# Stationary operands woven in pairs of blocks in a hybrid encoder layer

## Chip, cores and metric

The kernel runs on one core of a Trainium2 chip. The metric is the device time of one execution in microseconds.

## What is computed

One encoder layer over 512 tokens of width 1024 (two sequences of 256), all in float32: a token mixer of three branches, then a mixture of 16 experts of which each token uses two. Cut to its matrix products, the reference is

```python
z = x @ w_in + b_in                       # q, k, v, u_sg, v_sg, glu_a, glu_g
a = neighbourhood_attention(q, k, v, rpb) @ w_a_o
bb = (u * sv) @ w_b_o                     # u = gelu(u_sg); sv: position mixing of layer_norm(gelu(v_sg))
c = silu(layer_norm(depthwise_conv(glu_a * sigmoid(glu_g)))) @ w_c_o
g = sigmoid(x @ w_gate + b_gate)          # three gates of width 1024
merged = g[0] * a + g[1] * bb + g[2] * c
x = layer_norm(ALPHA * x + merged @ w_o + b_o)
...
for e in range(N_EXPERTS):
    h = silu(xt @ w_e1[e]) * (xt @ w_e3[e])
    y = y + gates[:, e:e + 1] * (h @ w_e2[e])
x = layer_norm(ALPHA * x + y)
```

## The kernel before

Every engine has its own program, written out by hand, and semaphores join them. All large products use float32 values split in two: `hi` is the value cast to the engine's float32r type, `lo` the rest, value minus `hi`. A product of two values takes three matmuls, written by `three` (lines 1842 to 1844): hi by hi, hi by lo, lo by hi. TensorE takes for each a stationary operand of 128 x 128, which a weight load (LDWEIGHTS) brings in, and a moving operand of 128 x 512, read from SBUF while the matmul runs.

Weights come in units of 128 x 1024 elements (512 KB). For each unit SyncE issues a transfer into a ring (`raw`, later with `raw_rows`, `raw_more`, `raw_late`: 24 slots), ScalarE casts it to `w_hi` (`cast_hi`, line 719), VectorE subtracts into `w_lo` (`cast_lo`, line 1055), and TensorE uses it in 24 matmuls (before the experts) or 6 (in them). There are three slots for split units, four in the expert stage, so that ScalarE waits for TensorE to finish with an earlier unit.

There are 64 + 8 units before the experts. In `features` (units 0 to 7 and 16 to 63: glu, q, k, u_sg, the three gates and the three branch projections) the weights are stationary, as blocks of 128 columns, and the tokens move (`xT`, `branch`). In `tokens` (units 8 to 15, v and v_sg; units 64 to 71, the output projection `w_o`, whose last three of four units per half are in `mix_out`; and all 192 units of the experts) the transposed tokens are stationary (`xT`, `mT`, `xgT`, `hT`) and the weights move. `first_units` is `features` for units 0 and 1.

An expert is 12 units: four of w_e1, four of w_e3 (`hidden`), four of w_e2 (`output`). Its 128 gathered token rows `xg` are turned by 8 transposes (line 2137) into two PSUM banks, from which ScalarE writes `xgT_hi` (`split_xg`, line 932) and VectorE `xgT_lo` (line 1541); `h` is turned by 4 (line 2152) and split into `hT_hi` and `hT_lo` (lines 943 and 1551). `keep_busy` (line 2097) runs spare matmuls while the router's results are awaited, `joint_slots` (line 2117) builds the lists of slots by small matmuls, and `form_sum` (line 2238) starts the last sum with float32 matmuls of the identity by `x1`.

The operands of the large matmuls start at multiples of 256 bytes (`LINE`). Before the change every one is laid out block after block, so that a stationary block is 128 elements in a row in each partition.

## Time and profile before

| | us |
|---|---|
| median of 3 runs | 778.98 |
| lowest and highest | 777.98, 779.29 |
| the profiled execution | 777.9 |
| its span | 776.1 |
| TensorE matmuls busy | 745.4 (96%) |
| weight loads busy | 616.5 (79%) |
| VectorE busy | 609.9 (79%) |
| ScalarE busy | 432.6 (56%) |

The span goes from the first instruction to the last; 1.8 us of the execution's own time lie around it. Matmuls are pipelined: a row's duration holds the way through the array too, so two neighbours overlap, and the pace of a stream is read from the starts. A weight load has rows of its own (PEld) and runs beside the matmul before it.

### The profile page before, as it was taken

How to read it: one execution, taken by the hardware profiler on the slowest of the kernel's cores; microseconds unless marked ns; L12 is line 12 of the kernel's file. 1: busy time of each engine (PE TensorE's matmuls, PEld its weight loads, DVE VectorE, ACT ScalarE, POOL GpSimd, SP SyncE). 2: the span in 40 equal slices, each digit the busy share in tenths (PEclk: the TensorE clock that was granted, in tenths of full speed). 3: DMA queues.
4: the chain of work that ended last, by engine and by line, in shares of the span. 5: the costliest groups of instructions: out<-in, count | busy, mean ns of one | idle time of the engine just before them, and what ended most of it. 6: DMA issues, size and time to landing. Idle time of an engine off the chain costs nothing.

```text
span 776.1 us, 10638 instructions
## 1 busy us (share of the span) xinstructions
PE 745.4 (96%) x3516; PEld 616.5 (79%) x3516; DVE 609.9 (79%) x827; ACT 432.6 (56%) x585; POOL 72.0 (9%) x96
## 2 busy tenths in 40 slices
PE   4999999999999999999999979999999999999995
PEld 3888877887888888888888857888888888888873
DVE  5799977777678857444348888999999999999977
ACT  5522235657322335422421456888888888888851
POOL 5000000000000000000011121111111111110314
PEclk9999999999999999999999989999999999999998
DMA  9744657232343452332388587999999999999682
GB/s 297 238 98 108 204 147 205 71 93 84 109 134 109 112 167 74 115 103 88 104 303 300 186 302 255 351 392 379 388 386 389 391 400 384 381 394 378 146 171 111
DMA packets 137489, 175.51 MB, mean 226 GB/s; under 512 B 15419, under 2 KB 75559, under 8 KB 137431
## 3 DMA queue, kind: packets, MB, share of 16 engines
q1 hardware_dynamic: 128896, 154.95, 58.8%
q0 software_dynamic: 7616, 19.34, 8.3%
q10 hardware_dynamic: 934, 0.69, 0.3%
q8 instruction: 23, 0.38, 0.2%
q14 instruction: 20, 0.16, 0.1%
HBM read 164.06 MB, written 19.11 MB: 236 GB/s over the span
## 4 chain that ended last, share of the span: by engine, by line
PE 85%; DVE 8%; DMA 2%; ACT 2%; SPq 2%; issue 1%; POOL 0%; DVEq 0%; ACTq 0%; POOLq 0%
PE bank L1842 25%; PE bank L1844 25%; PE bank L1843 25%; DVE w_lo L1055 2%; PE bank L2137 2%; DMA raw<-in_w_in_dram 2%; SPq L606 1%; DVE conv L1125 1%; DVE conv_odd L1125 1%; PE bank L2058 1%; PE bank L1837 1%; PE bank L2152 1%; PE bank L2238 1%; PE bank L1888 1%; PE bank L1904 1%
## 5 line engine op out<-in xcount | busy, mean ns | idle before, releaser
L1055 DVE TENSOR_TENSOR w_lo<-raw,w_hi 128x1024 fp32r<-128x1024 f32 x103 | 125.0, 1220 | 77.2 <-ACT w_hi L719 77.1
L719 ACT CAST w_hi<-raw 128x1024 fp32r<-128x1024 f32 x103 | 107.0, 1048 | 101.5 <-PE bank L1844 97.6
L1842 PE MATMUL bank<-xT_hi,w_hi 128*128 128x512 f32 x352 | 138.5, 393 | 2.7 <-DVE xT_lo L1093 1.5
L1844 PE MATMUL bank<-xT_hi,w_lo 128*128 128x512 f32 x352 | 137.1, 390 | 0.0
L1843 PE MATMUL bank<-xT_lo,w_hi 128*128 128x512 f32 x352 | 137.0, 389 | 0.0
L1842 PE MATMUL bank<-w_hi,xgT_hi 128*128 128x512 f32 x198 | 80.1, 405 | 1.0 <-issue 1.0
L1842 PEld LDWEIGHTS bank<-xT_hi,w_hi 128*128 128x128 f32 x352 | 66.1, 188 | 17.3 <-issue 3.1
L1844 PE MATMUL bank<-w_hi,xgT_lo 128*128 128x512 f32 x198 | 77.5, 391 | 0.0
L1843 PE MATMUL bank<-w_lo,xgT_hi 128*128 128x512 f32 x198 | 77.3, 390 | 0.0
L1844 PEld LDWEIGHTS bank<-xT_hi,w_lo 128*128 128x128 f32 x352 | 66.1, 188 | 14.0
L1843 PEld LDWEIGHTS bank<-xT_lo,w_hi 128*128 128x128 f32 x352 | 66.1, 188 | 13.4
L834 ACT ACTIVATE gate<-bank,vec 128x512 f32<-128x512 f32 x24 | 16.5, 689 | 83.2 <-PE bank L1844 83.2
L1055 DVE TENSOR_TENSOR w_lo<-raw_more,w_hi 128x1024 fp32r<-128x1024 f32 x40 | 48.2, 1221 | 5.7 <-ACT w_hi L719 5.4
L1055 DVE TENSOR_TENSOR w_lo<-raw_late,w_hi 128x1024 fp32r<-128x1024 f32 x40 | 48.2, 1220 | 4.1 <-ACT w_hi L719 3.9
L1125 DVE SCALAR_TENSOR_TENSOR conv<-conv_in,conv_col,conv 128x512 f32<-128x512 f32 x60 | 44.6, 744 | 0.0
L719 ACT CAST w_hi<-raw_more 128x1024 fp32r<-128x1024 f32 x40 | 41.2, 1049 | 4.5 <-PE bank L1844 4.5
L1844 PEld LDWEIGHTS bank<-w_hi,xgT_lo 128*128 128x128 f32 x198 | 37.2, 188 | 7.9
L1842 PEld LDWEIGHTS bank<-w_hi,xgT_hi 128*128 128x128 f32 x198 | 37.3, 188 | 7.8 <-issue 1.2
L719 ACT CAST w_hi<-raw_late 128x1024 fp32r<-128x1024 f32 x40 | 41.2, 1050 | 2.5 <-PE bank L1844 2.5
L1843 PEld LDWEIGHTS bank<-w_lo,xgT_hi 128*128 128x128 f32 x198 | 37.3, 188 | 6.6
L1125 DVE SCALAR_TENSOR_TENSOR conv_odd<-conv_in,conv_col,conv_odd 128x512 f32<-128x512 f32 x56 | 41.6, 744 | 0.0
L1055 DVE TENSOR_TENSOR w_lo<-raw_rows,w_hi 128x1024 fp32r<-128x1024 f32 x32 | 38.3, 1218 | 0.0
(289 smaller groups left out, 1530.9 us busy)
## 6 DMA issues: line engine op xcount, KB each, us to landing
raw_more<-in_w_e_dram SPq DMA_DIRECT2D x48, 512.0 KB, 7.0
raw<-in_w_e_dram SPq DMA_DIRECT2D x48, 512.0 KB, 7.9
raw_late<-in_w_e_dram SPq DMA_DIRECT2D x48, 512.0 KB, 7.1
raw_rows<-in_w_e_dram SPq DMA_DIRECT2D x48, 512.0 KB, 7.9
raw<-in_w_in_dram SPq DMA_DIRECT2D x28, 512.0 KB, 6.5
raw<-in_w_gate_dram SPq DMA_DIRECT2D x24, 512.0 KB, 3.7
y_scratch<-zeros SPq DMA_DIRECT2D x8, 512.0 KB, 5.3
raw<-in_w_o_dram SPq DMA_DIRECT2D x8, 512.0 KB, 3.8
```

The source lines that it names most:

```text
L606: sp.dma_start(v_win[:, seq, j, :], v_grid[:, WINDOW[j]:WINDOW[j] + KCOLS, :]).then_inc(v_windows, 16)
L719: act.copy(hi_slot(j), raw_slot(j)).then_inc(hi_cast, 1)
L834: act.activation(gate[:, n if n < 2 else r % 2, d, :], bank(name)[:], ACT.Sigmoid, bias=column(V_GATE + n * DC + 2 * r + d)).then_inc(free ...
L1055: dve.tensor_tensor(lo_slot(j), raw_slot(j), hi_slot(j).bitcast(F32), ALU.subtract).then_inc(lo_cast, 1)
L1125: o = dve.scalar_tensor_tensor(out=sum_, in0=shifted, scalar=conv_col[:, k, c:c + 1], in1=sum_, op0=ALU.mult, op1=ALU.add)
L1837: o = pe.transpose(bank(name)[:, k * P:(k + 1) * P], tile(k), ident)
L1842: pe.matmul(out, hi_l, hi_r, start=start, stop=False)
L1843: pe.matmul(out, hi_l, lo_r, start=False, stop=False)
L1844: return pe.matmul(out, lo_l, hi_r, start=False, stop=stop)
L1888: o = pe.matmul(bank(("attended", g))[:, j * P:(j + 1) * P], v_win[:, seq, j, hp * P:(hp + 1) * P], probsT[:, j * P:(j + 1) * P], start=Tr ...
L1904: o = pe.transpose(bank(name)[:, tokens_of(t)], x_in[:, t, c * P:(c + 1) * P], ident)
L2137: o = pe.transpose(psum[M_XT + half][:, k * P:(k + 1) * P], xg[:, q, c * P:(c + 1) * P], ident)
```

## The change

Each stationary operand is woven: of two neighbouring blocks of 128 x 128, block 0 takes the even elements of 256 and block 1 the odd ones. The tiles are declared `[pairs, 128, 2]` instead of `[blocks, 128]`, with the same bytes; `woven`, `chunk` and `by_chunk` give the views. Woven are the split weights of `features` (`is_stationary`), `mT_hi`, `xgT_hi`, `xgT_lo`, `hT_hi` and `hT_lo`. Not woven are `xT` (which moves in `features` and is stationary in units 8 to 15), `mT_lo`, and all weights that move. The casts and subtractions that write a woven tile write with a step of two elements and take their source in the old order; those of VectorE also read the `hi` part with that step. The number and the order of the instructions, their waits, and all transfers stay the same. The first of two woven blocks starts at a multiple of 256 bytes, the second 4 bytes further.

```diff
--- before.py
+++ after.py
@@ -233,8 +233,8 @@
     w_s = sb(first, "w_s_in", [4, P])
     first.close()
     late = ExitStack()
-    mT_hi = sb(late, "mT_hi", [DC, T], F32R, LINE)
-    mT_lo = sb(late, "mT_lo", [DC, T], F32R)
+    mT_hi = sb(late, "mT_hi", [DC // 2, T, 2], F32R, LINE)
+    mT_lo = sb(late, "mT_lo", [DC, T], F32R, LINE)
     branch_hi.append(sb(late, "branch2_hi", [WC, T], F32R))
     branch_lo.append(sb(late, "branch2_lo", [WC, T], F32R))
     gate = sb(late, "gate", [2, 2, T])
@@ -310,12 +310,12 @@
     y_last_hi = sb(over_xg, "y_last_hi", [D], F32R, LINE)
     over_xg.close()
     xg = sb(moe, "xg", [2, D])
-    xgT_hi = sb(moe, "xgT_hi", [2, DC, SLOTS], F32R, LINE)
-    xgT_lo = sb(moe, "xgT_lo", [2, DC, SLOTS], F32R, LINE)
+    xgT_hi = sb(moe, "xgT_hi", [2, DC // 2, SLOTS, 2], F32R, LINE)
+    xgT_lo = sb(moe, "xgT_lo", [2, DC // 2, SLOTS, 2], F32R, LINE)
     h_silu = sb(moe, "h_silu", [FF])
     h = sb(moe, "h", [FF])
-    hT_hi = sb(moe, "hT_hi", [4, SLOTS], F32R, LINE)
-    hT_lo = sb(moe, "hT_lo", [4, SLOTS], F32R, LINE)
+    hT_hi = sb(moe, "hT_hi", [2, SLOTS, 2], F32R, LINE)
+    hT_lo = sb(moe, "hT_lo", [2, SLOTS, 2], F32R, LINE)
     over_y = ExitStack()
     y_0 = sb(over_y, "y_0", [D])
     y_last_lo = sb(over_y, "y_last_lo", [D], F32R, LINE)
@@ -418,7 +418,7 @@
     out_stored = sem("out_stored")
-    last_hT_hi, last_hT_lo = xgT_hi[:, 0, 0:4, :], xgT_lo[:, 0, 0:4, :]
+    last_hT_hi, last_hT_lo = xgT_hi[:, 0, 0:2], xgT_lo[:, 0, 0:2]
     turned = [next_turned[:, 0], onehot[:, 1]]
     placed_hi, placed_lo = [y_next_hi, y_last_hi], [y_next_lo, y_last_lo]
@@ -510,6 +510,30 @@
     def lo_slot(j):
         s = j % SPLIT if j < U_MOE else (j - U_MOE) % M_SPLIT
         return w_lo[:, s, :] if s < SPLIT else w_lo_more[:, s - SPLIT, :]
+
+    def is_stationary(j):
+
+        return j < U_V or U_QK <= j < U_WO
+
+    def woven(slot):
+
+        return slot.rearrange("p (k n b) -> p k b n", b=2, n=P)
+
+    def split_of(slot, j):
+
+        return woven(slot) if is_stationary(j) else slot
+
+    def raw_of(j):
+
+        return raw_slot(j).rearrange("p (k b n) -> p k b n", b=2, n=P) if is_stationary(j) else raw_slot(j)
+
+    def chunk(tile, c):
+
+        return tile[:, c // 2, :, c % 2]
+
+    def by_chunk(tile):
+
+        return tile.rearrange("p k n b -> p k b n")
     def unit_of(slot, cols):
         return slot.rearrange("p (c n) -> p c n", n=cols)
@@ -716,7 +740,7 @@
                 act.wait_ge(unit_used, nth(j - M_SPLIT + 1, per, i))
             elif j >= SPLIT:
                 act.wait_ge(unit_used, nth(j - SPLIT + 1, per, i))
-            act.copy(hi_slot(j), raw_slot(j)).then_inc(hi_cast, 1)
+            act.copy(split_of(hi_slot(j), j), raw_of(j)).then_inc(hi_cast, 1)
@@ -838,7 +862,7 @@
             for c in (2 * r, 2 * r + 1):
                 act.wait_ge(merged_ready, c + 1)
-                act.copy(mT_hi[:, c, :], merged[:, c, :]).then_inc(merged_hi, 1)
+                act.copy(chunk(mT_hi, c), merged[:, c, :]).then_inc(merged_hi, 1)
         for r in range(4):
             for n in range(2):
@@ -929,8 +953,8 @@
         def split_xg(n, q):
             for half in range(2):
                 act.wait_ge(*m_filled(M_XT + half, n))
-                act.copy(xgT_hi[:, q, 4 * half:4 * half + 4, :],
-                         psum[M_XT + half][:].rearrange("p (c n) -> p c n", c=4)).then_inc(xg_hi, 1)
+                act.copy(by_chunk(xgT_hi[:, q, 2 * half:2 * half + 2]),
+                         psum[M_XT + half][:].rearrange("p (k b n) -> p k b n", k=2, b=2)).then_inc(xg_hi, 1)
         def silu(unit, n, h_before=None):
             act.wait_ge(unit_used, unit + 1)
@@ -940,7 +964,7 @@
         def split_hT(n, hT_hi=hT_hi[:]):
             act.wait_ge(*m_filled(M_HT, n))
-            act.copy(hT_hi.rearrange("p c n -> p (c n)"), psum[M_HT][:]).then_inc(hT_hi_done, 1)
+            act.copy(by_chunk(hT_hi), psum[M_HT][:].rearrange("p (k b n) -> p k b n", k=2, b=2)).then_inc(hT_hi_done, 1)
         def scale_y(unit, n, q, half):
@@ -1052,7 +1076,7 @@
         def cast_lo(j, per=0, i=None):
             dve.wait_ge(hi_cast, nth(j, per, i))
-            dve.tensor_tensor(lo_slot(j), raw_slot(j), hi_slot(j).bitcast(F32),
+            dve.tensor_tensor(split_of(lo_slot(j), j), raw_of(j), split_of(hi_slot(j).bitcast(F32), j),
                               ALU.subtract).then_inc(lo_cast, 1)
         def row_stats(x, t):
@@ -1080,9 +1104,10 @@
         dve.tensor_copy(conv_col[:].rearrange("p t c -> p (t c)"), bank("vectors")[:, V_ALL:V_ALL + TAPS * WC])
         dve.tensor_copy(vec[:], bank("vectors")[:, 0:V_ALL]).then_inc(frees("vectors"), 1)
         dve.wait_ge(*raw_there(0))
-        dve.tensor_copy(hi_slot(0), raw_slot(0)).then_inc(first_hi, 1)
+        dve.tensor_copy(woven(hi_slot(0)), raw_of(0)).then_inc(first_hi, 1)
         dve.wait_ge(first_hi, 1)
-        dve.tensor_tensor(lo_slot(0), raw_slot(0), hi_slot(0).bitcast(F32), ALU.subtract).then_inc(lo_cast, 1)
+        dve.tensor_tensor(woven(lo_slot(0)), raw_of(0), woven(hi_slot(0).bitcast(F32)),
+                          ALU.subtract).then_inc(lo_cast, 1)
         for c in range(DC):
             if c % 2:
                 dve.wait_ge(x0T_full, c + 1)
@@ -1299,7 +1324,7 @@
             for c in (2 * r, 2 * r + 1):
                 dve.wait_ge(merged_hi, c + 1)
-                dve.tensor_tensor(mT_lo[:, c, :], merged[:, c, :], mT_hi[:, c, :].bitcast(F32),
+                dve.tensor_tensor(mT_lo[:, c, :], merged[:, c, :], chunk(mT_hi, c).bitcast(F32),
                                   ALU.subtract).then_inc(merged_lo, 1)
         done = 80
@@ -1537,9 +1562,11 @@
         def split_xg(n, q):
             for half in range(2):
                 dve.wait_ge(xg_hi, n * 2 + (half + 1))
-                part_of = (slice(None), q, slice(4 * half, 4 * half + 4))
-                dve.tensor_tensor(xgT_lo[part_of], psum[M_XT + half][:].rearrange("p (c n) -> p c n", c=4),
-                                  xgT_hi[part_of].bitcast(F32), ALU.subtract).then_inc(psum_free[M_XT + half], 1)
+                part_of = (slice(None), q, slice(2 * half, 2 * half + 2))
+                dve.tensor_tensor(by_chunk(xgT_lo[part_of]),
+                                  psum[M_XT + half][:].rearrange("p (k b n) -> p k b n", k=2, b=2),
+                                  by_chunk(xgT_hi[part_of].bitcast(F32)),
+                                  ALU.subtract).then_inc(psum_free[M_XT + half], 1)
         def gate_h(unit, n):
             dve.wait_ge(unit_used, unit + 1)
@@ -1548,8 +1575,8 @@
         def split_hT(n, hT_hi=hT_hi[:], hT_lo=hT_lo[:]):
             dve.wait_ge(hT_hi_done, n + 1)
-            dve.tensor_tensor(hT_lo.rearrange("p c n -> p (c n)"), psum[M_HT][:],
-                              hT_hi.rearrange("p c n -> p (c n)").bitcast(F32),
+            dve.tensor_tensor(by_chunk(hT_lo), psum[M_HT][:].rearrange("p (k b n) -> p k b n", k=2, b=2),
+                              by_chunk(hT_hi.bitcast(F32)),
                               ALU.subtract).then_inc(psum_free[M_HT], 1)
         make_joint(0, 0)
@@ -1846,13 +1873,13 @@
         def features(j, outs, x_hi, x_lo, per=0, i=None):
             pe.wait_ge(lo_cast, nth(j + 1, per, i))
-            hi, lo = unit_of(hi_slot(j), len(outs) * P), unit_of(lo_slot(j), len(outs) * P)
+            hi, lo = woven(hi_slot(j)), woven(lo_slot(j))
             chunks = UNIT // (len(outs) * P)
             for d, name in enumerate(outs):
                 open_bank(name, i)
-                cols = slice(d * P, (d + 1) * P)
                 for c in range(chunks):
-                    o = three(bank(name)[:], hi[:, c, cols], lo[:, c, cols], x_hi[:, c, :], x_lo[:, c, :],
+                    at = (slice(None), *divmod(len(outs) * c + d, 2))
+                    o = three(bank(name)[:], hi[at], lo[at], x_hi[:, c, :], x_lo[:, c, :],
                               c == 0, c == chunks - 1)
             o.then_inc(unit_used, 1)
@@ -1862,7 +1889,7 @@
             hi, lo = unit_of(hi_slot(j), 512), unit_of(lo_slot(j), 512)
             for t, out in enumerate(outs):
                 for c in range(2):
-                    o = three(out, choose(x_hi[:, 2 * k + c, :], t), choose(x_lo[:, 2 * k + c, :], t), hi[:, c, :],
+                    o = three(out, choose(x_hi(2 * k + c), t), choose(x_lo(2 * k + c), t), hi[:, c, :],
                               lo[:, c, :], k == 0 and c == 0, last and c == 1)
             o.then_inc(unit_used, 1)
@@ -1892,6 +1919,15 @@
         def in_row(x, t):
             return x[:, tokens_of(t)]
+        def whole(x, t):
+            return x
+
+        def chunks_of(tile):
+            return lambda c: chunk(tile, c)
+
+        def rows_of(tile):
+            return lambda c: tile[:, c, :]
+
         pe.wait_ge(const_loaded, 16)
         def turn_x0(t, chunks):
@@ -1923,10 +1959,10 @@
             name = ("glu_g" if u else "glu_a", 0)
             if chunks[0] == 0:
                 open_bank(name)
-            hi, lo = unit_of(hi_slot(u), P), unit_of(lo_slot(u), P)
+            hi, lo = woven(hi_slot(u)), woven(lo_slot(u))
             for c in chunks:
                 pe.wait_ge(*drained(("x0T", c)))
-                o = three(bank(name)[:], hi[:, c, :], lo[:, c, :], xT_hi[:, c, :], xT_lo[:, c, :], c == 0,
+                o = three(bank(name)[:], hi[:, c // 2, c % 2], lo[:, c // 2, c % 2], xT_hi[:, c, :], xT_lo[:, c, :], c == 0,
                           c == DC - 1)
             if chunks[-1] == DC - 1:
                 o.then_inc(unit_used, 1)
@@ -1946,12 +1982,14 @@
                 if u == U_V:
                     for t in range(TT):
                         open_bank(("v", t))
-                tokens(u, u - U_V, u == U_V + 3, [bank(("v", t))[:] for t in range(TT)], xT_hi, xT_lo, in_row)
+                tokens(u, u - U_V, u == U_V + 3, [bank(("v", t))[:] for t in range(TT)],
+                       rows_of(xT_hi), rows_of(xT_lo), in_row)
             elif u < U_QK:
                 if u == U_VSG:
                     for t in range(TT):
                         open_bank(("vsg", t))
-                tokens(u, u - U_VSG, u == U_VSG + 3, [bank(("vsg", t))[:] for t in range(TT)], xT_hi, xT_lo, in_row)
+                tokens(u, u - U_VSG, u == U_VSG + 3, [bank(("vsg", t))[:] for t in range(TT)],
+                       rows_of(xT_hi), rows_of(xT_lo), in_row)
             elif u < U_USG:
                 features(u, [("k" if u % 2 else "q", (u - U_QK) // 2)], xT_hi, xT_lo)
             else:
@@ -2014,8 +2052,8 @@
                 open_bank(("mixed", n, t))
             for k in range(1 if n else 4):
                 pe.wait_ge(merged_lo, 2 * k + 2)
-                tokens(U_WO + 4 * n + k, k, k == 3, [bank(("mixed", n, t))[:] for t in range(TT)], mT_hi, mT_lo,
-                       in_row)
+                tokens(U_WO + 4 * n + k, k, k == 3, [bank(("mixed", n, t))[:] for t in range(TT)],
+                       chunks_of(mT_hi), rows_of(mT_lo), in_row)
         def mix_out(t):
@@ -2025,7 +2063,7 @@
                 pe.wait_ge(lo_cast, j + 1)
                 hi, lo = unit_of(hi_slot(j), 512), unit_of(lo_slot(j), 512)
                 for c in range(2):
-                    o = three(bank(name)[:], in_row(mT_hi[:, 2 * k + c, :], t), in_row(mT_lo[:, 2 * k + c, :], t),
+                    o = three(bank(name)[:], in_row(chunk(mT_hi, 2 * k + c), t), in_row(mT_lo[:, 2 * k + c, :], t),
                               hi[:, c, :], lo[:, c, :], False, k == 3 and c == 1)
             if t < TT - 1:
                 o.then_inc(fills(name), 1)
@@ -2143,7 +2181,7 @@
                 pe.wait_ge(*m_empty(b, n))
             if k % 2 == 0:
                 pe.wait_ge(*m_drained(M_XT + k // 2, n))
-            tokens(j, k, k == 3, [psum[b][:]], xgT_hi[:, q], xgT_lo[:, q], lambda x, t: x, per, i)
+            tokens(j, k, k == 3, [psum[b][:]], chunks_of(xgT_hi[:, q]), chunks_of(xgT_lo[:, q]), whole, per, i)
         def turn_h(n):
             pe.wait_ge(*m_empty(M_HT, n))
@@ -2158,7 +2196,7 @@
                 pe.wait_ge(*m_drained(M_HT, n))
             if k % 2 == 0:
                 pe.wait_ge(*m_empty(M_Y + k // 2, n))
-            tokens(j, k % 2, k % 2 == 1, [psum[M_Y + k // 2][:]], hT_hi, hT_lo, lambda x, t: x, per, i)
+            tokens(j, k % 2, k % 2 == 1, [psum[M_Y + k // 2][:]], chunks_of(hT_hi), chunks_of(hT_lo), whole, per, i)
         pe.wait_ge(routed, 1)
         joint_slots(0, 0)
```

## Rows read from the trace of the kernel before

**Rows 1.** The page: busy time of each engine; chain that ended last, by line

```profile
PE 745.4 (96%) x3516; PEld 616.5 (79%) x3516; DVE 609.9 (79%) x827; ACT 432.6 (56%) x585; POOL 72.0 (9%) x96
...
PE bank L1842 25%; PE bank L1844 25%; PE bank L1843 25%; DVE w_lo L1055 2%; PE bank L2137 2%; DMA raw<-in_w_in_dram 2%; SPq L606 1%; DVE conv L1125 1%; DVE conv_odd L1125 1%; PE bank L2058 1%; PE bank L1837 1%; PE bank L2152 1%; PE bank L2238 1%; PE bank L1888 1%; PE bank L1904 1%
```

**Rows 2.** Grouped instructions of TensorE: busy us, mean ns, idle before

```profile
L1842 PE MATMUL bank<-xT_hi,w_hi 128*128 128x512 f32 x352 | 138.5, 393 | 2.7 <-DVE xT_lo L1093 1.5 <-DVE vs L1217 1.0 <-DVE w_lo L1055 0.2
...
L1842 PEld LDWEIGHTS bank<-xT_hi,w_hi 128*128 128x128 f32 x352 | 66.1, 188 | 17.3 <-issue 3.1 <-DVE w_lo L1055 0.6 <-DVE xT_lo L1093 0.5
L2152 PEld LDWEIGHTS bank<-const,h 128*128 128x128 f32 x64 | 8.0, 141 | 2.1
```

**Rows 3.** Timeline of TensorE matmuls, 301 us: start, duration, instruction

```profile
300.69 0.39 PE L1843 MATMUL bank<-xT_lo,w_hi 128*128 128x512 f32 x1
...
302.28 0.39 PE L1844 MATMUL bank<-xT_hi,w_lo 128*128 128x512 f32 x1
```

**Rows 4.** Timeline of TensorE weight loads, same stretch

```profile
302.28 0.19 PEld L1842 LDWEIGHTS bank<-xT_hi,w_hi 128*128 128x128 f32 x1
```

**Rows 5.** Stretches: length, busy by engine, granted clock, DMA share, GB/s

```profile
300.00:303.00 3.00, 3.00 (x15) 2.48 (x14) 3.00 (x3) 0.00 (x0) 0.00 (x0) 1.00 0.07 15
463.20:465.70 2.50, 2.50 (x7) 1.98 (x6) 2.50 (x3) 0.00 (x0) 1.56 (x1) 0.50 0.57 167
```

**Rows 6.** Timeline of TensorE matmuls, 463 us

```profile
463.20 3.37 PE L2097 MATMUL bank<-w_hi 128*128 128x512 f32 x8
```

**Rows 7.** Timeline of TensorE matmuls, last sum

```profile
757.58 1.02 PE L2238 MATMUL bank<-x,const 128*128 128x512 f32 x2
...
759.82 0.59 PE L2238 MATMUL bank<-x,const 128*128 128x512 f32 x1
```

**Rows 8.** Timelines of TensorE at 474 us, matmuls, then weight loads

```profile
475.11 0.40 PE L1843 MATMUL bank<-w_lo,xgT_hi 128*128 128x512 f32 x1
...
476.51 0.39 PE L1843 MATMUL bank<-w_lo,xgT_hi 128*128 128x512 f32 x1
...
473.98 0.86 PEld L2117 LDWEIGHTS bank<-info,onehot 128*128 128x128 f32 x7
474.76 0.19 PEld L1842 LDWEIGHTS bank<-w_hi,xgT_hi 128*128 128x128 f32 x1
```

**Rows 9.** Timeline of TensorE matmuls, 483 us

```profile
483.53 0.39 PE L1843 MATMUL bank<-w_lo,xgT_hi 128*128 128x512 f32 x1
483.76 0.40 PE L1844 MATMUL bank<-w_hi,xgT_lo 128*128 128x512 f32 x1
...
485.83 0.39 PE L1842 MATMUL bank<-w_hi_more,xgT_hi 128*128 128x512 f32 x1
...
486.73 0.39 PE L1843 MATMUL bank<-w_lo_more,xgT_hi 128*128 128x512 f32 x1
```

**Rows 10.** Stretches of the first stage and the expert stage

```profile
20.00:125.00 105.00, 103.92 (x463) 85.91 (x464) 90.33 (x132) 33.71 (x42) 1.90 (x2) 1.00 0.58 164
500.00:550.00 50.00, 50.00 (x241) 41.66 (x239) 46.51 (x49) 42.71 (x52) 5.06 (x5) 1.00 1.03 386
```

**Rows 11.** Chain of waits, expert stage: turns of xg

```profile
513.21 0.87 PE bank L2137 x8
...
530.90 0.88 PE bank L2137 x8
```

**Rows 12.** Grouped instructions of VectorE and ScalarE

```profile
L1055 DVE TENSOR_TENSOR w_lo<-raw,w_hi 128x1024 fp32r<-128x1024 f32 x103 | 125.0, 1220 | 77.2 <-ACT w_hi L719 77.1
L1541 DVE TENSOR_TENSOR xgT_lo<-bank,xgT_hi 128x512 fp32r<-128x512 f32 x32 | 20.4, 676 | 0.0
...
L719 ACT CAST w_hi<-raw 128x1024 fp32r<-128x1024 f32 x103 | 107.0, 1048 | 101.5 <-PE bank L1844 97.6 <-DMA raw<-in_w_in_dram 3.9
L932 ACT CAST xgT_hi<-bank 128x512 fp32r<-128x512 f32 x32 | 17.2, 590 | 17.0 <-PE bank L2137 17.0
```

## The prediction

> **What bounds the kernel now.** I read the page first: TensorE is busy 96% of the span, and of the chain that ended last a quarter of the span lies on each of the three matmuls of `three` [rows 1]. So time is saved only by a shorter pace of these matmuls. The change touches none of their number, shape or order; it changes how their stationary operand lies in SBUF. All hangs on one question: does the weight load, which runs beside the matmul before it, cost that matmul anything?
>
> The grouped rows give a load of 188 ns beside a matmul of 393 ns [rows 2], but both overlap their neighbours, so a group's mean says nothing of the pace. The timeline does. In a steady stretch (300.69 to 302.28 us) seven matmuls start 1.59 us apart from first to last, 0.227 us each [rows 3], and each load starts as a matmul starts [rows 4]. 512 columns at 2.4 GHz, which is the clock granted there (1.00) [rows 5], are 213.3 ns. So 13.3 ns per matmul are something else, 6% of the pace.
>
> Two more stretches tell what it is. At the granted clock 0.50 (1.2 GHz) eight matmuls of the same form take 3.37 us; less the last one's 0.39, seven starts are 0.426 us apart, just 512/1.2, though loads run beside them too [rows 5, 6]. At full clock a pair of F32 matmuls of 512 columns (line 2238) lasts 1.02 us against 0.59 for one: 0.43 apart, twice 0.215, so two passes at the full rate of columns with nearly nothing on top [rows 7]. Both of these take their moving elements from SBUF half as fast. Thus the 13.3 ns are no fixed price of changing weights: they come only when the moving operand is read at full speed and a load reads beside it. The two reads hinder each other.
>
> How much they hinder is a matter of their position in time. After small matmuls seven of the same shape start 1.40 us apart from first to last, 0.233 each [rows 8]. Elsewhere, also behind small matmuls (the turns of h), the four steps from 485.83 to 486.73 take 0.225 each again [rows 9]. Operands and bytes are alike, so this is no toll per load; collisions of two moving pointers fit it.
>
> A load's own reading time: where small matmuls are bound by their loads (line 2117, seven of them, then the next matmul's), seven loads go by from 473.98 to 474.76, 0.11 us each [rows 8]; the 188 ns of a row are that and a latency. In 0.11 us a load reads 128 elements of 4 bytes, 4.8 bytes per ns; the matmul reads 4 bytes per 0.417 ns, 9.6 bytes per ns. The moving pointer overtakes the load's all the time.
>
> **The change, part by part.** *Woven loads.* `features` takes a woven stationary operand in 56 units of 24 matmuls, 1344 (1056 of them on xT, three times the 352 of [rows 2]); the output projection in 8 units of 24, but only for mT_hi, two of each three, 128; the experts in 192 units of 6, 1152. Sum 2624, of them 1472 before the expert stage. The 192 in which xT itself is stationary stay as they are. A woven load passes over 1,024 bytes in the same 0.11 us: 9.6 bytes per ns, the very speed of the moving pointer. Two pointers at one speed keep their distance. If they collide at the start the stalled one falls back and they are apart for the rest. I therefore forecast that most of the 13.3 ns goes. The floor is 214 ns, nearly the bare 512 columns, as in the passes of [rows 7]; the ceiling on this view is the 0.227 of now. I take 216, two ns above the floor for the first collision: 10.7 ns saved.
>
> No row shows a woven load, so I bound it. Below: 214, which is 12.7 x 2624 = 33 us less. Above: the nearest load at an equal pace is that of a turn (line 2152), contiguous but 141 ns long instead of 188 [rows 2]: 47 ns less of about 110, so it reads some 8 to 9 bytes per ns. The matmul that it runs beside, at 483.76, is 0.40 long where those before it are 0.39 [rows 9]: up to some 10 ns dearer, I take 6, so 19 ns of toll in little more than half the reading time. This row speaks against me, and it is the price of the rival below.
>
> *Before the expert stage*: 1472 x 10.7 = 15.8 us, all on the chain; DVE has 90.3 of 105 us in the busiest stretch and would have 90.3 of 100 (463 matmuls start there) [rows 10].
>
> *Expert stage*: an expert takes 17.69 us (turns of xg at 513.21 and 530.90) [rows 11]. 72 x 10.7 ns = 0.77 makes it 16.92. DVE is busy 46.5 of 50 us [rows 10], 0.93 to 0.94; 0.94 x 17.69 = 16.6 us per expert. That just fits, but each subtraction waits for ScalarE's cast and that for TensorE to free a slot, so DVE is late next. Of 1152 x 10.7 = 12.3 us I count 10. The transfers keep up: of ScalarE's idle time before its casts the group of ring `raw` names 3.9 us of waiting for a unit to land, and those from w_in alone [rows 12].
>
> *Writers.* ACT's cast (1048 ns) and DVE's subtraction (1220 ns) of 56 units of stationary weights now write, and DVE also reads, every second element; so do xgT (590 and 676 ns) and hT [rows 12]. No row has a step of two. Below: nothing, as a gain would need more than one element at a time from operands that lie worse than now. Above: twice the time per element, (1220 - 676)/512 = 1.06 ns each more. In 20 to 125 us eleven such units would add 12 us to DVE's 90 of 105, still hidden; per expert three splits of 512 would add 1.6 us to DVE's 16.6, which would stand out by 0.5 us, 8 us in all. I take nothing: these rows show one element at a time and nothing that a neighbour could save. The order of instructions, the waits, the DMAs and SBUF sizes stay as they are.
>
> Sum: 15.8 + 10 = 26 us. The profiled execution took 777.9 us, 752 after; the median of the runs is 1.1 us above it, so **753 us**.
>
> **The rivals.** *The load's reads are the toll (slower).* 512 contiguous bytes cost 13.3 ns. If each stretch of SBUF that a load opens stalls the matmul, a woven load opens twice as many: 26.6 ns, pace 240, 13.3 x 2624 = 35 us more, 814. By the turn's row, 19 ns in about half the time, it could be near 40 ns, 850. For it: the turn's row, and that the steady toll is so constant. Against it: equal loads cost 0.233 or 0.227 by position [rows 8, 9]. It decides from any pace above 227. The Trainium skill (SBUF — State Buffer, Door 1, the note on cachelines) says that SBUF is read in lines of 16 bytes and that each access that crosses to a new line pays, with at least two hits per line wanted. A woven load has two hits where it had four, so by that page it is at the edge of being free and may well pay here; the toll fits 32 lines per load, but no row tells lines from elements.
>
> *No meeting at all (no change).* The toll may follow the number of elements, or be part of handing over at full clock; then 227 stays and the time is 779. For it: elements and load count are unchanged. Against it: the 0.426 and 0.43 of the half-rate stretches [rows 6, 7]. The Trainium skill (TensorE: Matmul & The Clock Gate, Part 2, step 1) gives the engine two independent read ports and says that a load steals no read bandwidth from the running matmul: by that rule weaving does nothing. The 13.3 ns disagree with it.
>
> *Never settled (slower).* At equal speed a bad distance may be kept too, and the pace stay in the mix of [rows 8], 0.233: 6 x 2624 = 16 us more, 794.
>
> *The writers become the bound:* 8 us more, 787.
>
> **How the numbers follow.** Forecast 0.45, its own range 745 to 773 (214 ns to a saving of a few ns). No change 0.15. Toll doubled 0.28, never settled 0.09, writers 0.03. Faster is thus 0.45, the same 0.15, slower 0.40, where 0.2% (1.6 us) is about what a measurement tells from none. The range 747 to 816 leaves out 0.04 below and about half of the toll's case, 0.14, above.
>
> **What would show it.** Right: starts of woven matmuls 0.214 to 0.218 apart, while those with contiguous operands (`tokens` on xT, 192 of them) stay at 0.227; an expert of 16.9 to 17.1 us with DVE at 97% or more; load rows still 188 ns. Wrong: a pace of 0.227 everywhere (no meeting), of 0.240 or more in the woven ones alone (toll), or casts above 1.1 us for ACT and 1.3 us for DVE in woven units.

## The result and the profile after

| | before | after |
|---|---|---|
| median, us | 778.95 | 795.33 |
| lowest and highest | 777.98, 779.29 | 794.87, 795.59 |
| the profiled execution | 777.9 | 795.1 |
| its span | 776.1 | 793.3 |

The ratio is 1.0212, with a 95% interval of 1.0194 to 1.0229: the change costs 16.4 us. The table's time before is the median of four runs. The forecast was 753 us, 26 less than before. Its sign is wrong. The range (747 to 816) holds the result only because it was drawn wide enough for the rivals.

The page of the kernel after, TensorE's line and the chain that ended last by line (the three matmuls of `three` are now lines 1869 to 1871):

```profile
PE 762.3 (96%) x3516; PEld 634.4 (80%) x3516; DVE 611.3 (77%) x827; ACT 438.4 (55%) x585; POOL 71.8 (9%) x96
...
PE bank L1869 27%; PE bank L1871 27%; PE bank L1870 27%; PE bank L2175 2%; PE bank L2096 1%; PE bank L1864 1%; PE bank L2190 1%; PE bank L2276 1%; PE bank L1915 1%; DVE w_lo L1079 1%; PE bank L1940 1%; DMA x_in<-in_x_prompt_dram 1%; PE bank L1905 1%; PE bank L2135 1%; ACT w_hi L743 1%
```

As in [rows 1] TensorE is busy 96% of the span and the three lines hold 81% of it on the chain, where it was 75. The counts of instructions are those of before. Its busy time is 16.9 us longer, nearly the 17.2 us of the span: the whole loss is TensorE's own time.

The grouped rows of the same execution, matmuls and loads:

```profile
L1869 PE MATMUL bank<-xT_hi,w_hi 128*128 128x512 f32 x352 | 140.4, 399 | 3.1 <-DVE xT_lo L1118 1.8 <-DVE vs L1242 1.1 <-DVE w_lo L1079 0.2
...
L1869 PEld LDWEIGHTS bank<-xT_hi,w_hi 128*128 128x128 f32 x352 | 68.3, 194 | 17.8 <-issue 3.5 <-DVE w_lo L1079 0.6 <-DVE xT_lo L1118 0.4
```

Matmuls went from 393 to 399 ns in the first form [rows 2], and a load row from 188 to 194. What stands ahead of them as idle time is the same (2.7 us, now 3.1): no new wait.

The pace is read from starts. The timeline of TensorE's matmuls in three stretches: woven weights in `features`; `tokens` on xT, whose stationary operand the change left alone; and the experts, with woven xgT and hT.

```profile
302.74 0.39 PE L1869 MATMUL bank<-xT_hi,w_hi 128*128 128x512 f32 x1
...
305.77 0.40 PE L1870 MATMUL bank<-xT_lo,w_hi 128*128 128x512 f32 x1
...
80.11 0.39 PE L1869 MATMUL bank<-w_hi,xT_hi 128*128 128x512 f32 x1
...
83.96 0.39 PE L1871 MATMUL bank<-w_hi,xT_lo 128*128 128x512 f32 x1
...
499.66 0.40 PE L1870 MATMUL bank<-w_lo,hT_hi 128*128 128x512 f32 x1
...
504.79 0.39 PE L1871 MATMUL bank<-w_hi,xgT_lo 128*128 128x512 f32 x1
```

The first two rows are 13 starts apart, 3.03 us: **0.233 us** each, where [rows 3] have 0.227. The next two are 17 starts apart, 3.85 us: 0.2265, as before. The last are 22 apart, 5.13 us: 0.233. So the matmuls with woven loads got slower, by some 6.7 ns each, and those on xT did not. Over the whole trace, taking every pair of neighbours that follow each other at once, the mean step went from 227.2 to 233.4 ns in `features` on xT, from 227.8 to 233.9 in the experts' matmuls on xgT (three of four weight slots), and from 226.8 to 235.3 in those on hT, the dearest; on xT as the stationary operand it is 226.7 both times.

Two stretches (columns as in [rows 5]) and, from the chain of waits, the turns of xg:

```profile
20.00:125.00 105.00, 103.91 (x453) 85.91 (x454) 89.57 (x128) 33.67 (x40) 1.91 (x2) 1.00 0.57 162
500.00:550.00 50.00, 50.00 (x234) 42.09 (x233) 45.75 (x47) 42.00 (x51) 6.07 (x6) 1.00 1.02 371
```

```profile
505.18 0.87 PE bank L2175 x8
523.40 0.87 PE bank L2175 x8
```

The clock is granted in full (1.00) in both, as before. In the same 105 us 453 matmuls start instead of 463, in the expert stage 234 instead of 241 [rows 10]. An expert takes 18.21 us instead of 17.69 [rows 11]: 0.52 more, over its 72 matmuls 7.2 ns each. VectorE's share fell (46.51 to 45.75 us of 50): it has more slack, not less.

The writers of the woven operands, grouped:

```profile
L1079 DVE TENSOR_TENSOR w_lo<-raw,w_hi 128x1024 fp32r<-128x1024 f32 x103 | 125.2, 1222 | 84.5 <-ACT w_hi L743 83.5
L743 ACT CAST w_hi<-raw 128x1024 fp32r<-128x1024 f32 x103 | 111.4, 1091 | 102.8 <-PE bank L1871 99.3 <-DMA raw<-in_w_in_dram 3.5
L956 ACT CAST xgT_hi<-bank 128x512 fp32r<-128x512 f32 x32 | 18.4, 634 | 18.4 <-PE bank L2175 18.4
```

Against [rows 12]: VectorE's subtractions do not feel a step of two (1220 to 1222 ns, 676 to 679). ScalarE's casts do a little: 590 to 634 for xgT, and 1048 to 1091 in a group of which about half is woven, so some 80 ns for a woven unit (an estimate, 43 ns x 103 / 56). In 20 to 125 us ScalarE is busy 34 of 105 us, in the expert stage 42 of 50, so that this stays hidden.

### The profile page after: what moved, and what is told of

Read it like the earlier page. It is cut to its first block, busy times and chain, and to the rows that moved or that the text cites. A ratio compares the mean times of both kernels' runs of the same rounds, so it can differ in the third digit from the quotient of the medians.

```text
span 793.3 us, 10638 instructions
## 1 busy us (share of the span) xinstructions
PE 762.3 (96%) x3516; PEld 634.4 (80%) x3516; DVE 611.3 (77%) x827; ACT 438.4 (55%) x585; POOL 71.8 (9%) x96
## 4 chain that ended last, share of the span: by engine, by line
PE 92%; DVE 4%; ACT 2%; issue 1%; DMA 1%; POOL 0%; ACTq 0%; DVEq 0%; POOLq 0%
PE bank L1869 27%; PE bank L1871 27%; PE bank L1870 27%; PE bank L2175 2%; PE bank L2096 1%; PE bank L1864 1%; PE bank L2190 1%; PE bank L2276 1%; PE bank L1915 1%; DVE w_lo L1079 1%; PE bank L1940 1%; DMA x_in<-in_x_prompt_dram 1%; PE bank L1905 1%; PE bank L2135 1%; ACT w_hi L743 1%
## 5 line engine op out<-in xcount | busy, mean ns | idle before, releaser
L1079 DVE TENSOR_TENSOR w_lo<-raw,w_hi 128x1024 fp32r<-128x1024 f32 x103 | 125.2, 1222 | 84.5 <-ACT w_hi L743 83.5
L743 ACT CAST w_hi<-raw 128x1024 fp32r<-128x1024 f32 x103 | 111.4, 1091 | 102.8 <-PE bank L1871 99.3
L1869 PE MATMUL bank<-xT_hi,w_hi 128*128 128x512 f32 x352 | 140.4, 399 | 3.1 <-DVE xT_lo L1118 1.8
L1871 PE MATMUL bank<-xT_hi,w_lo 128*128 128x512 f32 x352 | 139.0, 395 | 0.0
L1870 PE MATMUL bank<-xT_lo,w_hi 128*128 128x512 f32 x352 | 138.9, 395 | 0.0
L1869 PEld LDWEIGHTS bank<-xT_hi,w_hi 128*128 128x128 f32 x352 | 68.3, 194 | 17.8 <-issue 3.5
L1871 PEld LDWEIGHTS bank<-xT_hi,w_lo 128*128 128x128 f32 x352 | 68.2, 194 | 14.0
L1870 PEld LDWEIGHTS bank<-xT_lo,w_hi 128*128 128x128 f32 x352 | 68.3, 194 | 13.3
L1079 DVE TENSOR_TENSOR w_lo<-raw_more,w_hi 128x1024 fp32r<-128x1024 f32 x40 | 48.2, 1222 | 7.1 <-ACT w_hi L743 6.4
L1079 DVE TENSOR_TENSOR w_lo<-raw_late,w_hi 128x1024 fp32r<-128x1024 f32 x40 | 48.2, 1222 | 5.7 <-ACT w_hi L743 4.7
L743 ACT CAST w_hi<-raw_more 128x1024 fp32r<-128x1024 f32 x40 | 41.1, 1048 | 4.8 <-PE bank L1871 4.8
```

The lines of the kernel that those rows point to most:

```text
L743: act.copy(split_of(hi_slot(j), j), raw_of(j)).then_inc(hi_cast, 1)
L1079: dve.tensor_tensor(split_of(lo_slot(j), j), raw_of(j), split_of(hi_slot(j).bitcast(F32), j), ALU.subtract).then_inc(lo_cast, 1)
L1869: pe.matmul(out, hi_l, hi_r, start=start, stop=False)
L1870: pe.matmul(out, hi_l, lo_r, start=False, stop=False)
L1871: return pe.matmul(out, lo_l, hi_r, start=False, stop=stop)
```

## Experiments

**Two theories at the start.** *Lines:* a woven load opens twice as many stretches of SBUF, each costing the running matmul something. *Position:* what counts is where a load stands against the moving operand, and "woven" is one position among others.

**b1_steps**, a bench: one weight block and one moving operand, both at multiples of 256 bytes, in a row of equal matmuls with nothing else running. It computes nothing of the layer, as the other benches below, and its time says nothing; only its timeline is read. Each loop is one case (written here in short), first steps 1 and 2; steps 3, 4, 8 and 16 follow, then 1 and 2 again with the stationary operand starting 1 to 192 elements on or the moving one 1 to 128:

```python
for k in range(16):
    o = pe.matmul(psum[1][:, 0:512], w[:, 0:128], x[:, 0:512], start=True, stop=True)
for k in range(16):
    o = pe.matmul(psum[2][:, 0:512], w[:, 0:255:2], x[:, 0:512], start=True, stop=True)
...
```

> A bench of the disputed cost alone: nothing of the layer is computed, two input tiles are split into one stationary and one moving tile, and stretches of 12 to 16 float32r matmuls of 512 columns follow each other, each stretch with another step or start of the stationary operand or start of the moving one. Toll by lines opened (32 per load of step 1, 64 of step 2, 96 of step 3, 128 from step 4 on): the pace depends on the step alone. With 226.7 ns at step 1 and 233.3 at step 2 as the kernels show, 6.7 ns per 32 lines: step 3 gives 240, steps 4, 8 and 16 give 246.7, whatever the starts. Pointers that meet by position: the starts matter, the pace changes by several ns when the stationary or the moving operand is shifted by 4 to 128 elements, and it does not grow evenly with the step; some start of step 2 is at 220 or below. At 256 and 128 moving columns the load has less to hide behind: 107 ns plus 106.7 and 112 as a bound by the load.

The timeline of the bench's matmuls, a row for each case. From one row's start to the next, over the count, is the pace:

```profile
22.24 3.79 PE L58 MATMUL bank<-x,w 128*128 128x512 f32 x16
25.87 3.90 PE L60 MATMUL bank<-x,w 128*128 128x512 f32 x16
29.61 3.92 PE L62 MATMUL bank<-x,w 128*128 128x512 f32 x16
33.37 3.92 PE L64 MATMUL bank<-x,w 128*128 128x512 f32 x16
37.13 4.09 PE L66 MATMUL bank<-x,w 128*128 128x512 f32 x16
41.06 3.93 PE L68 MATMUL bank<-x,w 128*128 128x512 f32 x16
44.82 3.80 PE L70 MATMUL bank<-x,w 128*128 128x512 f32 x16
...
59.60 2.96 PE L80 MATMUL bank<-x,w 128*128 128x512 f32 x12
62.41 2.96 PE L82 MATMUL bank<-x,w 128*128 128x512 f32 x12
...
92.89 2.92 PE L104 MATMUL bank<-x,w 128*128 128x512 f32 x12
95.65 2.92 PE L106 MATMUL bank<-x,w 128*128 128x512 f32 x12
```

Line 58, step 1: 3.63 / 16 = 0.227. Line 60, step 2: 3.74 / 16 = 0.234. The bench has both paces of the two kernels, with no other engine at work. Steps 3 (line 62) and 4 (64) give 0.235, step 8 (66) 0.246, step 16 (68) 0.235 again; line 70 is step 1 once more, 0.227 or a little above with its first matmul.

Its weight loads, grouped by line (columns as in [rows 2]):

```profile
L60 PEld LDWEIGHTS bank<-x,w 128*128 128x128 f32 x16 | 3.1, 193 | 0.6
...
L64 PEld LDWEIGHTS bank<-x,w 128*128 128x128 f32 x16 | 3.8, 309 | 0.0
```

With the step a load row itself grows: 188, 193, 253 (step 3), 309, 330 ns (step 8); yet step 4, whose row is 1.6 times that of step 2, has nearly step 2's pace. A toll per stretch opened, sized by the 6.7 ns between steps 1 and 2, would have put step 3 at 240 and steps 4, 8 and 16 all at 246.7. Step 8 alone comes near that.

Position does matter. A contiguous block that starts 16 elements on (64 bytes, line 80) has 2.81 / 12 = 0.234, with nothing woven. Over all starts tried at step 1: 0.227 at 0, 64, 128 and 192 elements, which are multiples of 256 bytes (at 128 after eight matmuls); 229 to 234 ns at 1, 2, 4, 8, 16, 24, 32, 48 and 96. A moving operand that starts 64 or 128 elements on leaves 0.227, one that starts 16 on gives 0.229, one that starts 1 on 0.2365. Step 2 is the other way round: 0.233 at 0, 64, 128 and 192, and as low as 0.230 at 16 (line 104: 2.76 / 12) and 24. No start brought it as low as 0.227.

**Each half of the change alone.** `e1_only_before_experts` lays xgT and hT block after block again:

```diff
-    xgT_hi = sb(moe, "xgT_hi", [2, DC // 2, SLOTS, 2], F32R, LINE)
+    xgT_hi = sb(moe, "xgT_hi", [2, DC // 2, 2, SLOTS], F32R, LINE)
...
-    hT_hi = sb(moe, "hT_hi", [2, SLOTS, 2], F32R, LINE)
+    hT_hi = sb(moe, "hT_hi", [2, 2, SLOTS], F32R, LINE)
```

> Woven operands in the first part and mT_hi only; the experts' tokens (xgT, hT) contiguous. If each woven matmul costs its 6.7 ns wherever it stands: 1472 x 6.7 = 9.8 us over the kernel before, 788.8, and the experts back at 17.69 us each. If the loss were made in the experts alone (their pace is 235.5, not 233.3): 779 to 781.

`e2_only_experts` keeps those woven and undoes the weights and mT_hi:

```diff
-        return j < U_V or U_QK <= j < U_WO
+        return False
...
-    mT_hi = sb(late, "mT_hi", [DC // 2, T, 2], F32R, LINE)
+    mT_hi = sb(late, "mT_hi", [DC, T], F32R, LINE)
```

> Woven operands in the experts alone; features and mT_hi as before. The rest of the loss: 18.2 against 17.69 us per expert, 15 to 16 experts, 7.7 us, 786.7. If the first part held all of it: 779 to 781. The two parts' losses should add up to the 16.4 us of the whole change.

| | median, us | ratio, 95% interval | loss |
|---|---|---|---|
| e1, before the experts only | 788.24 | 1.0119 (1.0100 to 1.0139) | 9.3 |
| e2, experts only | 785.75 | 1.0084 (1.0064 to 1.0104) | 6.8 |
| both (after) | 795.33 | 1.0212 (1.0194 to 1.0229) | 16.4 |

The losses are against 778.99, the median of before beside e1 and e2. The halves add up to 16.0. The timeline of e1, weights in `features`, then an expert:

```profile
302.75 0.39 PE L1871 MATMUL bank<-branch_hi,w_lo 128*128 128x512 f32 x1
...
305.78 0.39 PE L1869 MATMUL bank<-xT_hi,w_hi 128*128 128x512 f32 x1
...
508.28 0.39 PE L1871 MATMUL bank<-w_hi_more,xgT_lo 128*128 128x512 f32 x1
...
511.00 0.39 PE L1871 MATMUL bank<-w_hi,xgT_lo 128*128 128x512 f32 x1
```

13 starts in 3.03 us, 0.233; then 12 in 2.72, 0.2267. The slow pace goes with the woven stationary operand. (One group of e1's experts is slow with nothing woven: in the units of `w_hi_more` the mean step on xgT is 230.3 ns, against 226.9 before, with the same operands at the same addresses. What precedes a stretch has a part in its pace too, see e5.) And the count is right: 1472 x 6.7 ns = 9.8 us for the first half (9.3 measured), 1152 x 6.7 = 7.7 for the second (6.8).

**b2_map** asks what of the load hurts: how much it reads, how far it reaches, or where. It has a load that reads one element 128 times over (step 0), further steps, starts in fours, both operands shifted together, and loads of 64 and 32 columns.

```diff
-    w[:, 0:128]
+    w[:, 0:1].to_broadcast([P, P])
```

> A second bench of the same kind (nothing of the layer is computed): a load of step 0 (one element, one line), steps 5 to 31, starts of step 1 and step 2 from 0 to 64 elements in fours, both operands shifted together, loads of 64 and 32 columns, and a moving operand of one element repeated. If only the distance between the two read positions counts, shifting both operands together by 4 to 48 elements gives 226.7 and 233.3 again; if the place in SBUF counts by itself, other values. If the toll comes from meeting in SBUF at all, a moving operand that stays on one element or a load that stays on one element has another toll than one that runs; if it is a toll per element loaded, both have 13.3 ns, and loads of 64 and 32 columns have 6.7 and 3.3. Step 2 has no start below 226.7 on the first bench (best 230.0 at 24 elements); if equal speed could keep the pointers apart at some start, one of the seventeen starts is at 216 to 220.

The bench's timeline, contiguous, one element, step 5; then step 12 and the row after it:

```profile
22.51 3.79 PE L58 MATMUL bank<-x,w 128*128 128x512 f32 x16
26.14 3.87 PE L60 MATMUL bank<-x,w 128*128 128x512 f32 x16
29.84 3.97 PE L62 MATMUL bank<-x,w 128*128 128x512 f32 x16
...
41.27 4.45 PE L68 MATMUL bank<-x,w 128*128 128x512 f32 x16
45.55 4.22 PE L70 MATMUL bank<-x,w 128*128 128x512 f32 x16
```

A load of one single element gives 3.70 / 16 = 0.231: dearer than 128 in a row (0.227). This is fatal to lines, since a load that stays where it is opens none. Loads of 64 and 32 columns, a half and a quarter of the reading, give 0.230 and 0.232 (their rows 134 and 109 ns long). That is fatal to my two pointers, whose collisions last as long as the load reads: a quarter of the reading did not lower the toll. Of the steps only long ones leave the band of 227 to 235: 0.238 at 5 and 6, 0.239 at 7 and 31, 0.254 at 24, and at step 12 4.28 / 16 = 0.2675, where the load's row is 365 ns.

Of step 1's starts in fours only 0 and 64 have 226.7, and 4 and 60, the nearest to them, settle there after their first matmuls; all the others have 229 to 234. With both operands 8 to 48 elements on together the pace goes to 233.3 for step 2, and for step 1, once it settles, to 226.7 (at 16 in the last four of twelve matmuls, at 8 in the last two; at 32 and 48 only the last step of twelve is there). So it is mainly the **distance** between the two starts that counts, modulo 64 elements or 256 bytes: at step 2 a load 16 on beside a moving operand 48 on has 231.5, and a load 32 on 231.7; at step 1 a moving operand 16 on has the very cycle of 226, 229 and 232 ns of a load 48 on.

Two limits of that rule stand in the same traces. It holds for starts at multiples of 8 elements (32 bytes); below that the address counts too: both operands 4 on give 230.0 in turns of 227 and 233, and a moving operand 1 on gives 236.5 where a load 63 on, at the same distance, has 226.7 (b3). And one distance can have more than one pace, by what ran before it: 233.4 (b1) and 226.6 (b2) for step 1 at 4 elements, 233.3 (b3) and 226.7 (b4) at 61, 229.9 (b1) and 233.3 (b3) for step 2 at 24. With both operands at multiples of 256 bytes step 1 always came to 226.7, within nine matmuls, and step 2 to 233.3.

**e3_shift_contiguous** takes that to the kernel before: nothing woven, the same instructions, but the weight slots no longer at a multiple of 256 bytes. Two small tiles move from below them to ahead of them, and the slots no longer ask for the alignment:

```diff
-    w_hi = sb(ctx, "w_hi", [SPLIT, UNIT], F32R, LINE)
-    w_lo = sb(ctx, "w_lo", [SPLIT, UNIT], F32R, LINE)
+    neg_max = sb(ctx, "neg_max", [2, 4])
+    exp_sum = sb(ctx, "exp_sum", [2, 4])
+    w_hi = sb(ctx, "w_hi", [SPLIT, UNIT], F32R)
+    w_lo = sb(ctx, "w_lo", [SPLIT, UNIT], F32R)
```

> The kernel before, nothing woven, with w_hi and w_lo 64 bytes (16 elements) behind a multiple of 256. By the first bench a contiguous stationary operand there has a pace of 233.3, a contiguous moving one 229.0. 1344 matmuls of features x 6.7 = 9.0 us, 864 of the experts and some 384 before them x 2.3 = 2.9 us: 779.0 + 11.9 = 790.9. If the step, not the position, were what costs, this stays at 779.

The expectation had the address wrong: the slots came to lie 192 bytes (48 elements) past a multiple of 256, not 64. It took 788.58 us, ratio 1.0134 (1.0116 to 1.0151) to the 778.29 of before beside it: **10.3 us lost with nothing woven**. Its timeline, features and experts:

```profile
302.93 0.39 PE L1842 MATMUL bank<-xT_hi,w_hi 128*128 128x512 f32 x1
...
305.91 0.39 PE L1843 MATMUL bank<-xT_lo,w_hi 128*128 128x512 f32 x1
...
515.76 0.39 PE L1842 MATMUL bank<-w_hi,xgT_hi 128*128 128x512 f32 x1
...
518.33 0.39 PE L1844 MATMUL bank<-w_hi,xgT_lo 128*128 128x512 f32 x1
```

In features the load stands 48 past the moving operand: 2.98 / 13 = 0.229, which is b1's value for 48 (0.229). In an expert w_hi moves, so the load stands 48 behind, which is 16 modulo 64: 2.57 / 11 = 0.234, b1's value for 16. The two were expected the other way round, and the rule of the distance turns them round with the address. The fourth slot of the experts (`w_hi_more`) kept its place, and its units, at distance 0 but never more than six matmuls long, have a mean of 230.6.

**b3_columns** varies the length of the matmul, from 512 columns to 256, at steps 1 and 2, to see whether the toll grows with the columns. Two of the cases:

```diff
-    psum[1][:, 0:512], w[:, 0:128], x[:, 0:512]
+    psum[2][:, 0:508], w[:, 0:128], x[:, 0:508]
+    psum[7][:, 0:508], w[:, 0:255:2], x[:, 0:508]
```

> A third bench (nothing of the layer is computed): step 1 and step 2 at moving lengths of 256 to 512 columns, some starts at more lengths, starts one element apart, long stretches. All settled paces so far are whole numbers of 16 cycles of 2.4 GHz (226.7 ns = 34 x 16, 233.3 = 35 x 16, 120.0 at 256 columns = 18 x 16). If the toll is a wait for the next such slot at each handover, the pace goes in steps: 500, 504 and 508 columns cost the same as 512 or one slot of 6.7 ns less, 496 gives 220.0. If it is stalls spread over the load's reading, the pace falls by 0.417 ns with each column and the toll stays 13.3 (step 1) and 20.0 (step 2) at all lengths. One F32 matmul of 512 columns stays at 428 at both steps.

The rows for 256 columns at step 1, then 512, 508 and 504 at step 2:

```profile
60.91 2.08 PE L82 MATMUL bank<-x,w 128*128 128x256 f32 x16
62.83 3.88 PE L84 MATMUL bank<-x,w 128*128 128x512 f32 x16
66.54 3.79 PE L86 MATMUL bank<-x,w 128*128 128x508 f32 x16
70.18 3.79 PE L88 MATMUL bank<-x,w 128*128 128x504 f32 x16
```

| columns | 512 | 508 | 500 | 496 | 480 | 448 | 384 | 320 | 256 |
|---|---|---|---|---|---|---|---|---|---|
| step 1, ns | 226.7 | 227.6 | 223.4 | 223.3 | 216.6 | 202.6 | 173.3 | 146.7 | 120.0 |
| step 2, ns | 233.3 | 226.7 | 226.7 | 225.4 | 216.7 | 203.4 | 173.3 | 146.7 | 120.0 |

(Paces once they repeat, from the starts in the trace.) What lies above the bare columns at step 1 is 13.3 ns at 512 and at 256 alike (120.0 less 106.7) and up to 16.7 between: the toll is **one per matmul** and does not grow with columns. Neither picture of the expectation came out whole: the pace does not fall in plain slots (496 columns have 223.3, not 220.0), nor is the toll constant. And weaving costs something only near 512 columns: 6.7 ns there, 3.3 at 500 and 2 at 496, but nothing at 508, where it is 0.9 ns faster, and less than a nanosecond from 480 down in this table. Most paces that repeat without variation, 120.0, 146.7, 160.0, 173.3, 200.0, 226.7, 233.3, 240.0, are multiples of 6.67 ns, 16 cycles at 2.4 GHz: 18, 22, 24, 26, 30, 34, 35 and 36 of them. One is not: step 2 at 24 elements in b1 (line 106) stepped by 230 ns eleven times. The trace has two rows for each float32 matmul of 512 columns in the same bench, 429.2 ns apart at both steps, 2.5 ns above 1024 columns: there weaving costs nothing.

**e4_contiguous_64** and **e5_woven_64** put the weight slots 64 bytes past a multiple of 256, contiguous and woven, by this edit to the kernel before and to the kernel after:

```diff
+    moments = sb(ctx, "moments", [4, TT])
+    mv = sb(ctx, "mv", [TT, 2])
+    neg_max = sb(ctx, "neg_max", [2, 4])
+    exp_sum = sb(ctx, "exp_sum", [2, 4])
+    exp_inv = sb(ctx, "exp_inv", [2, 4])
-    w_hi = sb(ctx, "w_hi", [SPLIT, UNIT], F32R, LINE)
-    w_lo = sb(ctx, "w_lo", [SPLIT, UNIT], F32R, LINE)
-    const = sb(ctx, "const", [C_ALL], F32, LINE)
+    w_hi = sb(ctx, "w_hi", [SPLIT, UNIT], F32R)
+    w_lo = sb(ctx, "w_lo", [SPLIT, UNIT], F32R)
+    const = sb(ctx, "const", [C_ALL], F32)
```

> The kernel before, nothing woven, w_hi and w_lo 64 bytes behind a multiple of 256 (the run before this one had them 192 bytes behind it). Only the distance from the moving to the stationary operand, modulo 256 bytes, should count: features at +64 bytes 233.3 (they had 229 at +192), the experts and the units whose weights move at -64, which is +192: 229.0 (they had 233). 1344 x 6.7 = 9.0 us, 864 x 2.3 + 384 x 2.3 = 2.9 us: 778.6 + 11.9 = 790.5. If the place of w_hi by itself counted and not the distance, features and experts would be dearer by the same amount.

> The changed kernel, woven, with w_hi and w_lo 64 bytes behind a multiple of 256. By the first two benches a woven load at +64 bytes has 229.5 to 230.5 instead of 233.3: the 1344 matmuls of features win 3.3 ns each, 4.4 us; the experts' distance becomes +192, 233.2 on the bench, where they have 235.5 now: up to 2 us. 795.3 - 4.4 - 2 = 789 to 791. If position had no part in the woven pace, 795. Still slower than before, as no distance of a woven load reached 226.7.

The timelines in features, e4 first:

```profile
319.67 0.40 PE L1843 MATMUL bank<-branch_lo,w_hi 128*128 128x512 f32 x1
...
323.87 0.40 PE L1843 MATMUL bank<-xT_lo,w_hi 128*128 128x512 f32 x1
```

```profile
319.76 0.39 PE L1871 MATMUL bank<-xT_hi,w_lo 128*128 128x512 f32 x1
...
323.91 0.39 PE L1871 MATMUL bank<-xT_hi,w_lo 128*128 128x512 f32 x1
```

Both pairs are 18 starts apart. Contiguous: 4.20 us, 0.233 (0.227 at distance 0). Woven: 4.15 us, 0.2305 (0.233 at distance 0). The order is turned round in the kernel, as in the bench.

The times: e4 791.20 us, ratio 1.0158 (1.0141 to 1.0175), 12.5 us lost, 0.7 over what was expected. By the means of the trace that is 6.2 to 6.5 ns for each of the 1344 matmuls of `features`, and 2.2 to 5 ns for each of the experts' 1152, whose pace is 229.5 to 231.7. One part missed: in units 8 to 15, where xT is stationary and the weights move, 229 was expected and it is 233.3. e5 took 792.33, ratio 1.0180 (1.0163 to 1.0197), 3 us under the kernel after and 1.3 over the upper end of what was expected of it: `features` gained their 3.3 ns, while the experts' mean is still 232 to 233. Neither comes near before. A woven layout on the best distance found is dearer than a contiguous one on its best.

The part that missed shows what the distance leaves open. In units 8 to 15 the kernels e4 and e5 have the same contiguous operands at the same addresses; only the woven `features` units ahead of them differ. e4's timeline there:

```profile
80.18 0.40 PE L1844 MATMUL bank<-w_hi,xT_lo 128*128 128x512 f32 x1
...
83.68 0.40 PE L1844 MATMUL bank<-w_hi,xT_lo 128*128 128x512 f32 x1
```

15 starts in 3.50 us, 0.233, and 233.3 over all 191 steps. In e5 the 15 starts from 80.03 to 83.46 us are 0.229 apart, and 228.9 over all. So a whole stretch of 192 matmuls kept the pace in which it began, and what ran before it decided between the two.

**b4_moving** turns to the other side, the moving operand: it repeats its first m elements over the 512 columns, with loads of step 1, 2 and 0.

```diff
-    x[:, 0:512]
+    x[:, 0:1].to_broadcast([P, 512])
+    x[:, 0:16].unsqueeze(1).to_broadcast([P, 32, 16])
```

> A fourth bench (nothing of the layer is computed): the moving operand repeats its first 1, 2, 4, ... 256 elements to fill 512 columns, beside loads of step 1, step 2 and step 0 (one element). One element had 218.7 at both steps, the full operand 226.7 and 233.3. If the toll is the moving operand's own passage through SBUF at the hand-over, the pace depends on the moving pattern and hardly on the load: the same three numbers for steps 0, 1 and 2 within 7 ns, and a rise from 218.7 at some length of the repeated piece. If it is the two reads meeting, the pace stays at 218.7 while the moving operand stays in 16 or 64 bytes and the load passes it rarely, and step 0 differs from step 1 most where both stay. Fewer partitions (64, 32) or fewer stationary columns change nothing but the slot (226.7 to 233.3).

The rows of the full operand (lines 58 and 60), of m = 1 at steps 1, 2 and 0 (62, 64, 66), and of m = 16 at step 1 (86):

```profile
22.95 4.70 PE L58 MATMUL bank<-x,w 128*128 128x512 f32 x20
27.49 4.83 PE L60 MATMUL bank<-x,w 128*128 128x512 f32 x20
32.16 3.66 PE L62 MATMUL bank<-x,w 128*128 128x512 f32 x16
35.65 3.66 PE L64 MATMUL bank<-x,w 128*128 128x512 f32 x16
39.15 3.66 PE L66 MATMUL bank<-x,w 128*128 128x512 f32 x16
...
74.12 4.01 PE L86 MATMUL bank<-x,w 128*128 128x512 f32 x16
77.97 4.07 PE L88 MATMUL bank<-x,w 128*128 128x512 f32 x16
```

With m = 1 all three loads give 3.50 / 16 = 0.219, 5.4 ns above the bare columns; so do m = 2, 4 and 8, within a nanosecond. At m = 16 it is 3.85 / 16 = 0.241 at step 1 and 0.244 at steps 2 and 0, at m = 32 0.237, 0.240 and 0.2355; at m = 64 and more the full operand's paces are back, 0.227, 0.233 and 0.231 for steps 1, 2 and 0. So some 8 ns of the 13.3 come only with a moving operand that leaves its first 32 bytes, and only then does the load's layout matter at all. A load of one element has 231.1 at each of the starts 0, 16, 32 and 48: where the load does not move, the distance does not count. A load of 16 columns has 231.3. (The cases of 96 columns and of 32 partitions fell into a stretch at half clock and tell nothing.)

## Why the prediction was wrong

**Where it was right.** TensorE's pace was the whole question and every ns of it is on the chain. The matmuls that the change touches are the 2624 that I counted: the two halves, costed at 1472 and 1152, lost 9.3 and 6.8 us. `tokens` on xT stayed at 0.227. The writers added nothing that shows (TensorE's own 16.9 us are all but 0.3 of the span's growth), VectorE's rows did not move, and its slack grew, so "DVE is late next" was never put to the test.

**The step that failed** is "Two pointers at one speed keep their distance ... I therefore forecast that most of the 13.3 ns goes". I had 216 ns; it is 233.3. Not the size but the mechanism is wrong: the 13.3 ns are not made of collisions that last while the load reads. A load of a quarter of the columns has 232 (b2), one of an eighth 231 (b4), one of a single element 231, where the full load has 227. No step and no distance tried, more than 60 cases of full-length matmuls whose moving operand runs on through SBUF, came below 226.6: among the layouts of the load that were tried the gain that I forecast is not there.

Two readings led me there. [rows 6, 7] do show that at half the rate of columns nearly nothing lies on top, and b3's float32 matmuls bear this out (2.5 ns); but from "only at full rate" I went straight to "so two running reads collide", without asking what such collisions would do to a shorter load, though the turns' row [rows 9] already spoke against it: a shorter load with a dearer matmul. And I read the mix of 0.233 and 0.227 [rows 8, 9] as collisions that differ by position. But all those operands stand at the same distance, 0; the benches show such a mix for up to nine matmuls after a change of neighbours, before a contiguous load settles at 226.7. What position does was not in those rows. The 0.227 of the steady state was not a toll to be got rid of but the **best pace of several**, and before had it, because its operands start at multiples of 256 bytes and are contiguous. Weaving kept the addresses and lost the pace.

**What stands in its place**, as far as the runs show it. Each matmul of 512 columns with a load beside it pays 13 to 20 ns (steps 1 and 2), and it pays no less for a smaller load. How much goes by the load's step, its distance to the moving operand and, at distances other than 0, by what ran before. Where nothing varies, the pace came in slots of 6.67 ns (16 cycles) with the one exception above: a contiguous load at distance 0 modulo 256 bytes settles on 34 of them, a woven load on 35. Most other distances give cycles of several values, 229 to 234 in the mean. One slot times 2624 is 17.5 us; measured, 16.4 between medians and 17.2 between the spans. That the matmul beside a woven load pays more is shown, in the bench with no other engine at work; why it does is not.

**The rivals.** *Never settled*, with 0.09, forecast 794 us: 0.233 in the woven matmuls, and that is the size. That the size fits is luck in part: it took 0.233 for a bad distance that two pointers of equal speed may keep. For a woven load the bench has 0.233 at every multiple of 256 bytes, whatever ran before, so there was nothing better to settle on there; and the better distances (16 elements, e5 and b1) end at 0.230, still above a contiguous load's 0.227. No equal speed is needed either: a contiguous load 16 elements on keeps 0.233. But its idea that a pace, once taken, is kept is borne out by units 8 to 15 of e4 and e5. *The load's reads are the toll*, with 0.28, forecast 814 from a pace of 240, and is refuted by steps 3 and 4, no dearer than 0.235, and by the one-element load. The Trainium skill (SBUF — State Buffer, Door 1, the note on cachelines) has a penalty for each access that crosses to a new line; beside a load that never leaves its line the matmul pays 231 against 227, so that rule does not price this, though load rows that grow from 188 to 309 ns up to step 4 show that reading far apart does slow the load itself. *No meeting at all* fell: the pace changed by 2.9%. The Trainium skill (TensorE: Matmul & The Clock Gate, Part 2, step 1) says that a load takes no bandwidth from the running matmul. In so far as the amount loaded hardly matters (227 to 232 ns) the benches agree; that its layout then does not matter either, they contradict, with 226.7, 233.3 and 267 for steps 1, 2 and 12. *The writers become the bound* fell by the windows: VectorE 45.75 of 50 us.

**What stays open.** What in the chip has a period of 16 cycles and one of 256 bytes, and why a woven load at distance 0 lands just one slot later, no run tells. That a load is needed for the 5.4 ns that stay with a moving operand of one element was not tried. Nor do they tell what in the matmuls before picks one of two paces: the contiguous load 48 elements on had 229 in b1 and b2 and 233 in b3. Half the rate of columns is not enough by itself to be rid of the toll either, if b1's moving operand with a step of two is counted as such: it has 453 ns, 26 above 1024 columns. And the 235.3 of the experts' hT, 2 ns over the bench's woven pace, is unexplained. No version here beats the kernel before.

## What to carry to other kernels

Where matmuls with changing weights run back to back on float32r operands, start stationary and moving operands at the same offset modulo 256 bytes and keep a stationary block contiguous: that gave 226.7 ns for 512 columns every time, once settled. A few starts next to it reached that only in some stretches, and everything else tried with a full moving operand had 229 to 268, with nothing in the instructions to show for it. A constant excess over the bare columns is not by itself a loss that can be won back; before designing against it, vary its supposed cause by a large factor (a load of one element, a quarter of the columns) in a bench of a few microseconds per case. When a change moves addresses of a tuned kernel, even of small tiles declared ahead of the operands, compare the starts of twenty matmuls with those of before.

## What the runs showed of the hardware

- Declaring two small tiles ahead of the weight slots, with their alignment given up, cost 10.3 us of 778 (e3): a shift of addresses alone, 1.3%.
- The pace of equal matmuls often locks to a multiple of 16 cycles and keeps that over dozens of them (in b3 226.7 ns over 23 steps, 233.3 over 47).
- The same operands at the same addresses ran at 233.3 ns in e4 and 228.9 in e5 for 192 matmuls, behind different ones.
- A weight load of one repeated element hurts more than one of 128 in a row (231 and 227 ns), and at 508 columns, or at 384 and fewer in b3's table, the woven load costs nothing over the contiguous one.
- Load rows by step, in ns: 188, 193, 253, 309 for 1 to 4, 330 for 8, 300 for 16, 365 for 12.
- A moving operand read with a step of two takes 453 ns for 512 columns, twice the time, at either layout of the load (b1). The moving side is the one that must not be woven.
- ScalarE's write with a step of two costs 44 ns of 590; VectorE's costs 3 of 676.
